# Hybrid block on one core: exponentials of a pair queued behind the copy of the first turned row, value units evicted unscaled by ScalarE

## What is computed

```
h = rmsnorm(x) * g;  z = h @ w_in_2            # 512 x 3886, cut into pools, queries, keys, values, gates
# fox heads (6):  s = q k^T / 8 + F[t] - F[s], causal;     p = softmax(s);  o = p v
# dsa heads (6):  s = q k^T / 8, only the 128 keys with the highest index score;  p = softmax(s);  o = p v
# four pooled windows of 256 channels beside them
mixed = [pool * silu(pg), o_dsa * silu(dg), o_fox * silu(fg)]
x = x + mixed @ w_out_2;  out = rmsnorm(x)
```

## Time and profile before

| | us |
|---|---|
| median of 3 runs (1310.92 to 1311.26) | 1310.95 |
| the profiled execution, its own time | 1310.9 |
| its span, first to last instruction | 1309.2 |
| TensorE busy | 1288.6 (98%) |
| weight loads busy | 1028.6 (79%) |
| VectorE busy | 828.8 (63%) |
| ScalarE busy | 575.3 (44%) |
| GpSimd busy | 249.1 (19%) |

### The profile page before, as it was taken

One profiled execution on the slowest core, in us unless ns is written; L12 is line 12 of the kernel. 1 busy time (PEld: TensorE's weight loads), 2 busy tenths in 40 slices (PEclk: granted clock), 3 DMA queues, 4 the chain that ended last, 5 costly groups with the idle time before them and its releaser, 6 DMA issues.

```text
span 1309.2 us, 20297 instructions
## 1 busy us (share of the span) xinstructions
PE 1288.6 (98%) x6833; PEld 1028.6 (79%) x6833; DVE 828.8 (63%) x1715; ACT 575.3 (44%) x997; POOL 249.1 (19%) x484
## 2 busy tenths in 40 slices
PE   8999999999999999999999999999999999999998
PEld 6777878878788788888788888888877766767686
DVE  6976666676676753444477763477766688885723
ACT  5654535445454432223344432244454455555422
POOL 2513304033140300001200000000023023366300
PEclk9999999999999999999999999999999999999999
DMA  6323232232232223333233323333234322222221
GB/s 184 90 66 89 80 88 79 73 88 79 74 88 77 71 83 92 96 96 106 79 106 96 92 82 97 114 96 96 66 91 117 91 89 81 80 66 65 65 65 65
DMA packets 210051, 114.43 MB, mean 87 GB/s; under 512 B 7696, under 2 KB 206671, under 8 KB 210005
## 3 DMA queue, kind: packets, MB, share of 16 engines
q1 hardware_dynamic: 210005, 113.84, 30.0%
HBM read 111.70 MB, written 2.13 MB: 87 GB/s over the span
## 4 chain that ended last, share of the span: by engine, by line
PE 89%; DVE 7%; issue 2%; ACT 1%; DMA 0%; SPq 0%; DVEq 0%; POOLq 0%; ACTq 0%; POOL 0%
PE gb L671 75%; PE gb L1150 2%; PE gd L1150 1%; PE gd L1101 1%; PE gd L1078 1%; PE gd L1091 1%; DVE wlo L1624 1%; DVE selb L2191 1%; PE gd L779 1%; PE gd L871 1%; PE gd L862 1%; PE gd L767 0%; PE gd L850 0%; PE gd L851 0%; DVE selb L2202 0%
## 5 line engine op out<-in xcount | busy, mean ns | idle before, releaser
L671 PE MATMUL gb<-act_a,whi 128*128 128x512 f32 x2656 | 898.2, 400 | 2.5 <-DVE wlo L1624 2.5
L671 PEld LDWEIGHTS gb<-act_a,whi 128*128 128x128 f32 x2656 | 498.9, 188 | 121.3 <-issue 17.0
L671 PE MATMUL gb<-act_a,wlo 128*128 128x512 f32 x1416 | 552.3, 390 | 0.0
L1624 DVE TENSOR_TENSOR wlo<-raw,whi 128x1024 fp32r<-128x1024 f32 x189 | 236.0, 1249 | 149.1 <-ACT whi L1182 148.3
L1182 ACT ACTIVATE whi<-raw 128x1024 fp32r<-128x1024 f32 x211 | 223.2, 1058 | 216.9 <-PE gb L671 186.4
L671 PEld LDWEIGHTS gb<-act_a,wlo 128*128 128x128 f32 x1416 | 266.6, 188 | 48.3 <-issue 1.0
L671 PE MATMUL gb<-act_b,whi 128*128 128x512 f32 x432 | 152.5, 393 | 0.1
L671 PEld LDWEIGHTS gb<-act_b,whi 128*128 128x128 f32 x432 | 81.1, 188 | 17.4 <-DVE qc L1901 0.5
L2439 POOL TENSOR_TENSOR zs<-zs,ca 128x512 f32<-128x512 f32 x3 | 5.5, 1838 | 322.1 <-ACT ca L1185 322.1
L2471 POOL TENSOR_TENSOR wlo<-raw,whi 128x1024 fp32r<-128x1024 f32 x22 | 53.1, 2413 | 57.4 <-ACT whi L1182 57.4
L671 PE MATMUL gb<-act_b,wlo 128*128 128x512 f32 x128 | 49.9, 390 | 0.0
(11 more groups left out here) (467 smaller groups left out, 1558.9 us busy)
## 6 DMA issues: line engine op xcount, KB each, us to landing
raw<-in_w_in_dram SPq DMA_DIRECT2D x102, 512.0 KB, 3.4
raw<-in_w_up_dram SPq DMA_DIRECT2D x44, 512.0 KB, 3.6
raw<-in_w_down_dram SPq DMA_DIRECT2D x16, 384.0 KB, 3.1
raw<-in_w_down_dram SPq DMA_DIRECT2D x16, 320.0 KB, 3.1
raw<-in_w_a_out_dram SPq DMA_DIRECT2D x8, 512.0 KB, 3.4
raw<-in_w_b_out_dram SPq DMA_DIRECT2D x8, 512.0 KB, 3.4
raw<-in_w_o_dram SPq DMA_DIRECT2D x8, 512.0 KB, 3.4
raw<-in_w_out_dram SPq DMA_DIRECT2D x8, 512.0 KB, 3.5
```

Source lines behind the costliest of these rows:

```text
L671: ins = pe.matmul(gb[:, b, :], l, r, start=(first and m == 0), stop=(last and m == len(todo) - 1))
L1624: dve.tensor_tensor(wlo[:, i % 2, 0:k * P], raw[:, i % 4, 0:k * P], whi[:, i % 2, 0:k * P].bitcast(F32), ALU.subtract).then_inc(split_read ...
```

## The change

Four edits, all in the second block:

1. A new step `exp` stands in slot S + 4 place + 1 with order number 1, so behind a `t` in the same slot (0). ScalarE takes the exponentials of a pair there, and does nothing at `s` any more. TensorE, VectorE and GpSimd have no part in `exp` and keep their order of `s`.
2. The reciprocals of both heads are one VectorE instruction of two columns in the even head's `weigh`, which waits for both exponentials. The odd head's `weigh` only multiplies.
3. Value units are evicted by ScalarE with a plain copy. VectorE has no part in it, and waits before the eviction of the next unit until ScalarE has counted up `z_read`.
4. The copy of the turned values is made of four ScalarE instructions of 128 columns, each with its token factor as scale (tokens lie on partitions after the turn).

```diff
                 todo.setdefault(start + 4 * n, []).append((3, ("s", c, t)))
+                todo.setdefault(start + 4 * n + 1, []).append((1, ("exp", c, t)))
 ...
-                if what in ("g", "pg"):
+                if what == "v":
+                    sc.wait_ge(unit_done, N_Z + u + 1)
+                    sc.wait_ge(z_read, u)
+                    if g:
+                        sc.wait_ge(v_turn_done, g)
+                    sc.activation(vraw[:], gb[:, u % 4, :], ACT.Copy).then_inc(z_read, 1)
+                elif what in ("g", "pg"):
 ...
-                    sc.activation(flat(vt[g % 2]), gd[:, 2, :], ACT.Copy).then_inc(v_ready, 1)
-                elif what == "s":
+                    for c in range(TC):
+                        ins = sc.activation(vt[g % 2][:, c, :], gd[:, 2, c * P:c * P + P], ACT.Copy, scale=rr[:, 5, c:c + 1])
+                    ins.then_inc(v_ready, 1)
+                elif what == "exp":
 ...
-                    dve.wait_ge(exp_ready, n + 1)
-                    link(dve.reciprocal(small[:, 24 + k:25 + k], small[:, 12 + k:13 + k]))
+                    if t % 2 == 0:
+                        dve.wait_ge(exp_ready, n + 2)
+                        link(dve.reciprocal(small[:, 24 + k:26 + k], small[:, 12 + k:14 + k]))
 ...
+                if what == "v":
+                    return
                 src = gb[:, u % 4, :]
                 dve.wait_ge(unit_done, N_Z + u + 1)
+                if u and Z_UNITS[u - 1][0] == "v":
+                    dve.wait_ge(z_read, u)
 ...
-                elif what == "v":
-                    if g:
-                        dve.wait_ge(v_turn_done, g)
-                    ins = scale(vraw)
```

## The result

| | us | ratio to the kernel before (95% interval) |
|---|---|---|
| before, median of 12 runs (1310.92 to 1311.45) | 1311.08 | |
| after, median of 12 runs (1313.48 to 1315.43) | 1313.89 | 1.0024 (1.0017 to 1.0032) |
| after, the profiled execution, its own time | 1313.73 | |
| its span | 1312.0 | |

The changed kernel is slower by 2.8 us between the medians, 0.21%; the ratio in the table has 0.24%, and its interval lies clear of 1. The prediction of 1310.5 is 3.4 us too low, and the time is 0.7 above the end of its range. The 12 times after lie at two levels: seven between 1313.48 and 1313.92, with a mean clock of 0.997 or 0.998, and five between 1315.05 and 1315.43, all with 0.996. The profiled execution is of the lower level.

What follows compares the result with a forecast made beforehand. The prediction took TensorE as the bound and counted only its stops in the second block. The terms summed to -0.39 us, from the profiled 1310.9 to 1310.5 us, with a range of 1308.2 to 1313.2 us.

Steps and rivals of the forecast that it cites:

- first pair's stop, with unit 8's start: Group 0, first pair: exponentials wait behind Silu and table load, so TensorE's second products come later, +2.54 us.
- stop at the weighing, at the copy: Group 0, first pair's two turns: the stops behind VectorE's weighing and ScalarE's copy go, -0.93 and -0.86 us.
- last place of group 0: The split moves ahead of the exponentials, the copy ends earlier, and TensorE's stop goes entirely, -1.51 us.
- groups 1 and 2: Place 0: table load and exponentials, in group 2 also a split, delay the turn of the values, +0.8 and +1.7 us.
- groups 3 and 4: Place 0: the same table load is exposed but with shorter work around it, 0.1 us each, +0.2 in the sum.
- turns of group 3: An odd head's turn: the weighing, without its reciprocal, ends near 1168.6 and TensorE starts earlier, -0.6 us.
- odd turns of group 5: With the exponentials behind the even head's copy, both stops at odd heads' turns go, -1.73 us.
- the weighing is late, not the copy: Rival, 8%: at four odd turns the weighing becomes the last thing, so 3.84 us is not gained: 1314.4 us.
- The Silu held the pair: Third rival, 8%, denied this: first pair not held, its place -1.46 us instead of +0.75, total 1308.3 us.
- The loads do not stay hidden: First rival, 12%, claimed they do: the +0.8, +1.7 and +0.2 fall away, 1307.8 us.
- No switch cost more than its load row: A rival, 2%, claimed more: ScalarE idle between load and use, 0.6 to 1.4 us at five places, 1313.5 to 1317.5.

Runs made afterwards that it cites:

- The fourth experiment: The changed kernel with 13 matmuls whose result nobody reads on TensorE, ahead of its wait for the first pair's exponentials: 1312.52 us.
- second experiment: The changed kernel with the exponentials of place 1 of groups 1 to 5 put back ahead of the copy that waits for the product with the values: 1311.01 us.
- sixth experiment: The kernel before with only the exponentials' new slot and the shared reciprocal, values still evicted by VectorE: 1317.07 us.
- seventh kernel: The changed kernel, exponentials of group 0's first pair and of place 1 in groups 1 to 5 put back, gate 0's Silu moved to unit 11: 1306.77 us.
- first experiment: The changed kernel with the exponentials of group 0's first pair put back in slot S, ahead of the gate's Silu: 1311.37 us.
- fifth kernel: The kernel before with only the value edits: ScalarE evicts value units and applies the token factor in four copies: 1310.73 us.
- experiments 1, 3 and 4: Number 3: the changed kernel with exponentials of both the first pair and place 1 of groups 1 to 5 put back: 1307.8 us.
- tenth: The seventh kernel with one reciprocal for each head again, each waiting for its own exponential: 1307.38 us.

## Why the prediction was wrong

Its terms beside the jumps measured in after, each in us:

| term of the sum | predicted | measured | of the difference |
|---|---|---|---|
| first pair's stop, with unit 8's start | +2.54 | +2.86 | 0.18 is clock |
| half clock behind the stop | none | +1.36 | 1.36 is clock |
| stop at the weighing, at the copy | -0.93, -0.86 | -0.95, -0.86 | |
| last place of group 0 | -1.51 | -1.17 | |
| groups 1 and 2 | +0.8, +1.7 | +0.86, +1.77 | |
| groups 3 and 4 | +0.2 | +0.30 | |
| turns of group 3 | -0.6 | +0.15 | |
| odd turns of group 5 | -1.73 | -1.42 | |
| small ones, not in the sum | 0 | -0.30 | |
| sum | -0.39 | +2.60 | |

(The measured jump at the weighing is -0.61, since the turn itself took 0.34 longer at the half clock; the table counts the 0.34 in the row above. The 0.15 of group 3 is nothing at the odd turn of place 1, which the prediction had at -0.6, -0.11 at the even turn ahead of it and +0.26 at the odd turn of place 2, whose weighing of 384 columns takes 1.25 us instead of 0.42 beside GpSimd.)

**The step that failed first** is "TensorE then stands longer here. +2.54", and in it the price of a stop as its length. I found the length to 0.14 us (2.86 less the 0.18 of clock is 2.68). The 0.14 is the eviction's place, taken as 0.60 us of VectorE and worth 0.44: without it the next instruction on line 2191, `selb<-zs`, starts 0.86 us behind the start of the one ahead of it, where it was 1.27 with the eviction between them. But I took the work behind the stop as running as before. Its clock halved for 3.4 us and that cost 1.54 us, half of the miss of 2.99. The whole place came to +2.41 instead of +0.75, beyond the end of +1.5 that I gave it. The fourth experiment shows it: the same stop, filled, at a clock of 1.00, gives 1312.5, which is inside the range. I had read the mean clock of 0.999 of the kernel before and stopped there; but TensorE has no stop of this length anywhere in this kernel (the longest idle time between its first and its last matmul is the 1.32 of the earlier trace rows), so its trace could not show the price of one, and that was the unknown to be bounded. The Trainium skill (TensorE: Matmul & The Clock Gate, Why this matters for your kernels) warns of idle gaps between bursts of matmuls because the clock falls back behind them. The trace of after agrees, and the rule spoke against this change; it was not weighed.

**The second level of times** fits the same cause. In the profiles of the second and sixth kernels the half clock lasted 6.8 us, and the jump at the return is then +3.86 or +3.87 instead of +3.30, with more behind it: 1.1 and 1.2 us more in all. The medians of the levels of after are 1.5 apart, those of the second kernel 1.1. It was not seen in a profile of after itself, whose profiled run is of the lower level, so this is an inference from two other kernels. What chooses between 3.4 and 6.8 us in one and the same kernel stays open.

**The second step that failed** is "without its reciprocal of some 0.2 it ends near 1168.6", and with it the 1.73 of group 5 in full. I took the 0.55 of the weighing in the earlier trace rows for its own duration. It was a collision already: GpSimd's instruction ended at 1168.61 and the weighing at 1168.75. Wherever a weighing of 256 columns started within or just ahead of a `TENSOR_TENSOR` of GpSimd (by 0.01 us, in group 3), it ended 0.14 to 0.16 us behind it, however early it started: 1173.16 behind 1173.01, 1232.69 behind 1232.53, 1226.17 behind 1226.01, 1146.10 behind 1145.95, 1115.04 behind 1114.89. An earlier weighing gains nothing there unless it gets clear ahead of GpSimd, as in the seventh kernel with its 0.19, and a shift of the two lists against each other makes a new collision elsewhere. The Trainium skill (SBUF — State Buffer, Who interferes with whom) describes this as a port pair that one of the two holds for a whole instruction while the other waits. The trace agrees with its number: the wait ends with the instruction and is not a slowing in proportion. The rival "the weighing is late, not the copy" was therefore right in kind at two of the four turns, for a reason that it did not name, and cost 1.06 of the miss (0.75 and 0.31), not 3.84. It also was one of the signs that I had named for being wrong, a turn behind a weighing.

**The third** is "so the stop of 1.32 + 0.19 goes entirely". I set ScalarE's chain against the clock and let only TensorE come later. But the exponentials at its head wait for maxima of TensorE's own products: the first starts at 1091.89 instead of 1089.45, 2.44 later, when TensorE is 2.66 late. A delay of TensorE carries such a chain with it, and what remains is what the chain itself lost. From the first exponential to the Silu it takes 2.76 us instead of 3.72: 0.96, the split of 1.05 less the overlap of its row. And VectorE's first maximum starts 1.30 us behind the products instead of 1.50, since with the value edits VectorE is idle when they are ready: 0.20. This is the 1.17, and it was 1.16 or 1.17 in the first four experiments too, whose shifts just ahead of this point lie between -0.01 and +3.92. The fifth and the sixth have its two parts alone, -0.22 by the value edits and -0.95 by the order.

**What held.** The Silu held the pair, as the earlier trace rows had it; that rival is out. The loads do not stay hidden (+0.86, +1.77); that one is out too, and the second experiment took exactly these jumps away. No switch cost more than its load row: the load ends at 1066.57 and the exponential starts at 1066.59. The drain of about 1380 ns that the Trainium skill gives (ScalarE: Activation LUTs, What ACT_TABLE_LOAD costs) does not show after either; the measurement decides. The weighing's stop and the copy's went to 0.02 of the forecast. The moves of the evictions cost nothing in the kernel before, but the sixth experiment shows that they were not idle in the changed one.

**The range.** It took in the ends of each term, but for the one unknown that the trace did not show (what TensorE does behind a stop of 3 us) it had no end at all. The chances have a slip as well: 12% for the first rival and half of the third's 8% make 0.16 for faster and 0.74 for the same, not 0.14 and 0.76.

## What to carry to other kernels

A stop of the engine that bounds the kernel is not priced by its length once it is longer than any in the trace: the clock may fall, and here that added half of its length, so first fill such a stop or take it away (experiments 1, 3 and 4). When an order is changed for a gain in many places, look for those where it makes a new stop and leave them as they were. Here the first pair and place 1 of the later groups were such places; each alone brought the kernel back to the time before, and both together turned +2.8 us into -3.65, and -4.45 with one pair of table loads less. A short VectorE instruction whose row is longer than that of its sisters is probably waiting for GpSimd, and making it start earlier gains nothing until it starts clear ahead of GpSimd's.

## What the runs showed of the hardware

- Behind an idle time of TensorE of 2.91 to 2.92 us, in three kernels out of three, the granted clock was 0.50 for 3.4 us (after) or 6.8 us (the second and sixth kernels). In after it fell when TensorE was back at work, at 1068.70, 1.3 us behind the start of the products; in the other two it fell within the idle time, 0.45 and 0.22 us ahead of them. Idle times of 1.32 us (kernel before), 1.59 (after and the first experiment, at the values of group 2) and 1.62 (fourth and sixth) had no such effect: the clock stayed at 1.00.
- Matmuls on data nobody reads, put into the stop, kept the clock at 1.00 and made the kernel faster by 1.4 us (1.7 against the kernel before of the same runs), although TensorE had 13 matmuls more to do.
- At the half clock a unit matmul takes 0.43 us of TensorE's time instead of 0.23, and a turn of four squares 0.70 instead of 0.36.
- VectorE's `TENSOR_SCALAR` of 128 x 256 took 0.35 us alone, and also when it started 0.19 us ahead of GpSimd's `TENSOR_TENSOR` (seventh kernel, 1112.10). Behind the latter's start, or 0.01 us ahead of it, it took 0.42 us (fifth kernel, 1142.69) to 2.53 us (tenth, 1112.51), until 0.14 to 0.16 us behind the latter's end.
- ScalarE's table load took 1.28 us in each place, and an instruction behind it that waited for nothing else started 0.01 to 0.02 us later.
